# Inputs loaded transposed and split from SBUF, the memory block moved behind the projection, and the bias table read in its used order

## What is computed

```python
h, mem_n = rms_norm(x, pre_mix_g), rms_norm(mem, mem_norm_g)      # mem: 256 x 1024
q_n, k_c, v_c, k_s, v_s, k_w, v_w, g_n, q_m, k_m, v_m, q_x, gates = split(h @ w_in)
mk, mv = split(mem_n @ w_mem_kv)                                  # 4 heads of 64
# NSA, 8 heads in 2 groups: compressed, selected and window branch, each with
#   softmax(q k^T / 8 + bias_tab[t5_bucket(t - s)]) v, weighted by sigmoid(g_n)
# compress(k) = gelu((windows of 32 of k + pos) @ w1) @ w2, 15 windows
# MoBA, 4 heads, causal, same bias table (32 buckets x 12 heads); memory attention, 4 heads, no bias
merged = sum(sigmoid(gate_i) * (branch_i @ w_i_o))
x = x + rms_norm(merged @ w_mix_out, post_mix_g)
h = rms_norm(x, pre_ffn_g)
x = x + rms_norm((silu(h @ w_gate) * (h @ w_up)) @ w_down, post_ffn_g)
```

## Time and profile before

| | |
|---|---|
| median of 3 runs | 458.23 us (457.31 to 458.83) |
| the profiled execution | 457.53 us, its span 455.7 us |
| PE busy | 438.6 us (96% of the span) |
| DVE, ACT, POOL busy | 275.2, 240.5, 48.9 us |
| granted TensorE clock, mean | 0.997 of full |
| HBM read and written | 76.4 and 1.07 MB, 170 GB/s over the span |

### The profile page before, as it was taken

One profiled execution on the slowest core, in us unless ns is written; L12 is line 12 of the kernel. 1 busy time (PEld: TensorE's weight loads), 2 busy tenths in 40 slices (PEclk: granted clock), 3 DMA queues, 4 the chain that ended last, 5 costly groups with the idle time before them and its releaser, 6 DMA issues.

```text
span 455.7 us, 5968 instructions
## 1 busy us (share of the span) xinstructions
PE 438.6 (96%) x2096; PEld 351.9 (77%) x2096; DVE 275.2 (60%) x476; ACT 240.5 (53%) x412; POOL 48.9 (11%) x80
## 2 busy tenths in 40 slices
PE   3999999989999999999999989999999999999995
PEld 3776889977777777777778768888888888888883
DVE  2773893699565656754696666555555555545433
ACT  4673952377765556563436648444444444534321
POOL 5030000002112121120610230000000000000000
PEclk9999999999999999999999999999999999999998
DMA  8899825253534422335655364766555665555102
GB/s 283 312 377 324 265 89 186 92 177 100 180 98 119 159 95 92 94 95 182 235 180 185 118 205 147 236 188 186 189 183 187 189 184 184 180 182 184 74 0 92
DMA packets 50880, 77.79 MB, mean 171 GB/s; under 512 B 2068, under 2 KB 27372, under 8 KB 50856
## 3 DMA queue, kind: packets, MB, share of 16 engines
q1 hardware_dynamic: 49272, 73.07, 49.0%
q0 software_dynamic: 1424, 4.34, 2.9%
q10 hardware_dynamic: 160, 0.07, 0.1%
HBM read 76.40 MB, written 1.07 MB: 170 GB/s over the span
## 4 chain that ended last, share of the span: by engine, by line
PE 90%; DVE 3%; ACT 2%; DMA 2%; issue 1%; POOL 0%; POOLq 0%; SPq 0%; DVEq 0%; ACTq 0%
PE acc L1104 25%; PE acc L1106 24%; PE acc L1105 24%; PE ob L1351 3%; PE sbank L1274 2%; PE ptb L1325 2%; DMA mems<-in_mem 2%; PE ob L1258 2%; PE ob L1353 1%; PE sbank L1275 1%; PE ptb L1430 1%; ACT wh L459 1%; PE ob L1340 1%; DVE wl L728 1%; DVE gates L940 1%
## 5 line engine op out<-in xcount | busy, mean ns | idle before, releaser
L728 DVE TENSOR_TENSOR wl<-raw,wh 128x1024 fp32r<-128x1024 f32 (+1 forms) x130 | 158.7, 1227 | 84.8 <-ACT wh L459 84.1
L459 ACT ACTIVATE wh<-raw 128x1024 fp32r<-128x1024 f32 (+1 forms) x130 | 135.3, 1046 | 94.6 <-PE acc L1106 87.1
L1104 PE MATMUL acc<-wh,xh 128*128 128x512 f32 (+1 forms) x384 | 152.1, 396 | 0.2 <-DVE xl L758 0.2
L1106 PE MATMUL acc<-wh,xl 128*128 128x512 f32 (+1 forms) x384 | 148.6, 387 | 0.0
L1105 PE MATMUL acc<-wl,xh 128*128 128x512 f32 (+1 forms) x384 | 148.1, 386 | 0.0
L1106 PEld LDWEIGHTS acc<-wh,xl 128*128 128x128 f32 x384 | 72.1, 188 | 15.0
L1104 PEld LDWEIGHTS acc<-wh,xh 128*128 128x128 f32 x384 | 72.2, 188 | 14.4 <-issue 1.4
L1105 PEld LDWEIGHTS acc<-wl,xh 128*128 128x128 f32 x384 | 72.3, 188 | 13.3 <-issue 0.5
L1104 PE MATMUL acc<-wh,ah 128*128 128x512 f32 x88 | 34.9, 397 | 0.0
L1106 PE MATMUL acc<-wh,al 128*128 128x512 f32 x88 | 34.9, 396 | 0.0
L1105 PE MATMUL acc<-wl,ah 128*128 128x512 f32 x88 | 34.8, 396 | 0.0
(11 more groups left out here) (215 smaller groups left out, 466.3 us busy)
## 6 DMA issues: line engine op xcount, KB each, us to landing
raw<-in_w_in SPq DMA_DIRECT2D x20, 1024.0 KB
raw<-in_w_ffn_gate SPq DMA_DIRECT2D x22, 512.0 KB
raw<-in_w_ffn_up SPq DMA_DIRECT2D x22, 512.0 KB
raw<-in_w_ffn_down SPq DMA_DIRECT2D x22, 512.0 KB
raw<-in_w_mix_out SPq DMA_DIRECT2D x4, 1024.0 KB
bp<-g_scratch SPq DMA_DIRECT2D x1, 2304.0 KB, 8.5
raw<-in_w_nsa_o SPq DMA_DIRECT2D x2, 1024.0 KB
raw<-in_w_in SPq DMA_DIRECT2D x2, 560.0 KB
```

Of the source, the lines that this page charges most:

```text
L459: nc.scalar.activation(wh[:, k, :, 0:w], raw[:, slot, 2 * half:2 * half + 2, 0:w], ACT.Copy).then_inc(hi_done, 1)
L728: nc.vector.tensor_tensor(wl[:, k, :, 0:w], raw[:, slot, 2 * half:2 * half + 2, 0:w], wh[:, k, :, 0:w].bitcast(F32), ALU.subtract).then_in ...
L1104: nc.tensor.matmul(bank[:, 0:w], h[:, k, c], wh[:, slot, s, 0:w], start=first, stop=False)
L1106: return nc.tensor.matmul(bank[:, 0:w], l[:, k, c], wh[:, slot, s, 0:w], start=False, stop=last)
```

## The change

- **Inputs.** `x` and `mem` are also given transposed (`xt`, `memt`), the gains as columns (`gains`), the positions transposed (`post`). The splits read `xt0` and `memt0` in SBUF; PE's transposes of them, of the gains and of the positions are gone. `x0` and `mems` are still loaded, for the sums of squares, which ACT and DVE now take one token tile each.
- **Order of the blocks.** The projection becomes blocks 0 to 4 (subs 0 to 19, block 4 with 280 columns), memory keys and values block 5 (subs 20 to 23). The batches of queries and keys move with them: those of the projection are 0 to 6, that of the memory keys is the last, behind the first gate sub. `compress_1`, `compress_2` and the compressed scores move into block 5.
- **Bias table.** The row has 256 distances behind 127 masked ones; SP loads it back as `tb` directly (1.5 MB), the adds read it backwards, POOL copies the compressed branch's values out of it. The table products and their copies are gone, and `w1` waits for block 0 instead of `bp`.
- **First sub** in two pieces of one row group, each with loads and splits of its own.

```diff
# SP
-            for c in range(2):
-                sp.dma_start(mems[:, :, SLICE * c:SLICE * c + SLICE],
...
+            for s in range(2):
+                sp.dma_start(raw[:, 0, s], w_in[:, s, 0:SLICE]).then_inc(sub0d[s], 16)
+            sp.dma_start(xt0[:, 2:4], xt[:, 2:4]).then_inc(xtd[2], 16)
+            sp.dma_start(raw[:, 0, 2:4], w_in[:, 2:4, 0:SLICE]).then_inc(loaded[0], 32)
+            sp.dma_start(xt0[:, 4:8], xt[:, 4:8]).then_inc(xtd[3], 16)
+            plain(1, w_in, 4, 0)
+            plain(2, w_in, 0, SLICE)
+            plain(3, w_in, 4, SLICE)
             sp.dma_start(x0[:], xf).then_inc(xd, 16)
...
+            projection(2)
             sp.wait_ge(grow_done, 2)
             sp.dma_start(g_scratch, grow[:]).then_inc(g_stored, 16)
+            sp.dma_start(memt0[:], memt).then_inc(memtd, 16)
+            projection(3)
+            sp.dma_start(mems[:], memf).then_inc(memd, 16)
+            projection(4)
             sp.wait_ge(g_stored, 16)
-            sp.dma_start(bp[:], bass.AP(g_scratch.tensor, 0, [[1, P], [G_W, BIAS_H], [1, BP_W]])).then_inc(bp_d, 16)
+            sp.dma_start(tb[:], bass.AP(g_scratch.tensor, 0, [[1, P], [G_W, BIAS_H], [1, SEQ]])).then_inc(tb_d, 16)
# POOL
-            pool.wait_ge(bp_d, 16)
+            pool.wait_ge(mm_done, 4)
...
+            pool.wait_ge(tb_d, 16)
+            pool.wait_ge(zeroed, 3)
+            for t, seen in ((0, 7), (1, NCMP)):
+                src = tb[:, 0:NSA_H, 96 + P * t:97 + P * t]
+                nc.gpsimd.tensor_copy(tbc[:, t, :, 0:seen],
+                                      bass.AP(src.tensor, src.offset, [src.ap[0], [SEQ, NSA_H], [-CMP_STRIDE, seen]])
+                                      ).then_inc(tbc_done, 1)
# ACT
+            nc.scalar.dma_start(gcol[:], a["gains"]).then_inc(gaind, 16)
+            for s in range(2):
+                nc.scalar.dma_start(xt0[:, s], xt[:, s]).then_inc(xtd[s], 16)
...
+            for s in range(2):
+                x_hi(s)
+                first_hi(s)
+            split[0] = 1
+            for v in range(1, 4):
+                x_hi(2 * v)
+                x_hi(2 * v + 1)
+                hi_to(v)
+            hi_to(6)
+            act.wait_ge(xd, 16)
+            squares_of(1, x0, 0)
...
             evac_cols(2)
+            hi_to(15)
+            act.wait_ge(memtd, 16)
+            for k in range(4):
+                mem_hi(k)
+            hi_to(16)
+            high_qk(3)
+            for k in range(4, KD):
+                mem_hi(k)
             evac_cols(3)
             hi_to(20)
+            act.wait_ge(memd, 16)
+            squares_of(0, mems, 0)
+            act.wait_ge(ssq_done, 4)
+            roots(0)
+            nc.scalar.preload_act_table(ACT.Tanh)
             high_qk(4)
             evac_cols(4)
+            high_qk(5)
...
             hi_to(24)
             high_qk(6)
+            act.wait_ge(cmp_dve, 1)
+            nc.scalar.activation(hx[:, 2, :], hx[:, 1, :], ACT.Tanh, ...).then_inc(cmp_act, 1)
             evac_cols(5)
# DVE: the same order with x_lo, first_lo, mem_lo, lo_to, low_qk; the gelu stands behind low_qk(6)
-                            nc.vector.tensor_tensor(sx[:, n % 2, c0:c1], sbank[:, n % 2, c0:c1], tb[:, bh, 128 * (1 - t):256],
+                            nc.vector.tensor_tensor(sx[:, n % 2, c0:c1], sbank[:, n % 2, c0:c1], tb[:, bh, c1 - c0 - 1::-1],
# PE
+            def first_sub():
+                for s in range(2):
+                    pe.wait_ge(hi_done, s + 1)
+                    for t in range(TILES):
+                        nc.tensor.matmul(acc[:, 0, t], xh[:, s, P * t:P * t + P], wh[:, 0, s], start=(s == 0), stop=False)
+                    pe.wait_ge(xl_done, s + 1)
+                    pe.wait_ge(lo_done, s + 1)
+                    for t in range(TILES):
+                        nc.tensor.matmul(acc[:, 0, t], xh[:, s, P * t:P * t + P], wl[:, 0, s], start=False, stop=False)
+                        ins = nc.tensor.matmul(acc[:, 0, t], xl[:, s, P * t:P * t + P], wh[:, 0, s], start=False, stop=False)
+                ins.then_inc(mm_done, 1)
...
+            first_sub()
+            whole_block(0, 0, 4, xh, xl, ready=x_ready, after={1: [relative_bias]}, first=1)
+            whole_block(1, 4, 4, xh, xl)
+            whole_block(2, 8, 4, xh, xl, after={0: [lambda: qk_batch(0, 1, [col(C_Q), col(C_Q + P)])],
+                                                1: [lambda: qk_batch(1, 1, [col(C_Q + 2 * P), col(C_Q + 3 * P)])],
+                                                3: [lambda: qk_batch(2, 2, [col(C_KC), col(C_VC)])]})
+            whole_block(3, 12, 4, xh, xl, after={1: [lambda: qk_batch(3, 3, [col(C_KS), col(C_KW)])]})
+            whole_block(4, 16, 4, xh, xl, w=ATT_TAIL,
+                        after={1: [lambda: qk_batch(4, 4, [col(C_QM), col(C_QM + P)])],
+                               3: [lambda: qk_batch(5, 4, [col(C_KM), col(C_KM + P)])]})
+            whole_block(5, 20, 4, memh, meml, ready=mem_ready,
+                        after={0: [lambda: compress_1(0), lambda: compress_1(1)],
+                               1: [lambda: compress_1(2), lambda: qk_batch(6, 5, [col(C_QX), col(C_QX + P)])],
+                               2: [compress_2],
+                               3: [lambda: compressed_scores(0), lambda: compressed_scores(1)]})
```

More of the change, by code:

```diff
@@ L146, in build_layer @@
         xh = sb("xh", [P, KD, SEQ], F32R)
+        with ExitStack() as early:
+            xt0 = sb("xt0", [P, KD, SEQ], F32, early)
         xl = sb("xl", [P, KD, SEQ], F32R)
@@ L158, in build_layer @@
             memh = sb("memh", [P, KD, SEQ], F32R, s)
+            with ExitStack() as early:
+                memt0 = sb("memt0", [P, KD, SEQ], F32, early)
             meml = sb("meml", [P, KD, SEQ], F32R, s)
             mems = sb("mems", [P, TILES, D], F32, s)
[L161 to L165, removed]
         gates = sb("gates", [P, TILES, 3 * D])
@@ L340, in _ @@
+            for half in range(2):
+                plain(2 * B_MEMKV + half, w_memkv, 4 * half, 0)
+            u = 2 * B_GATE
             for gate_blocks, w in (((0, 1, 2, 3), w_moba), ((4, 5), w_mem)):
@@ L788, in _ @@
-            dve.wait_ge(memd[0], 16)
-            dve.wait_ge(memd[1], 16)
-            for t in range(TILES):
-                round_lo(1, t)
-                nc.vector.tensor_tensor_reduce(out=junk[:, t], in0=mems[:, t], in1=mems[:, t], scale=1.0, scalar=0.0, op0=ALU.mult,
-                                               op1=ALU.add, accum_out=ssq[:, 0, t:t + 1]).then_inc(ssq_done, 1)
-            lo_to(4)
-            for j in (2, 3):
-                round_lo(1, j)
+            for s in range(2):
+                x_lo(s)
+                first_lo(s)
@@ new lines, in _ @@
+            split[0] = 1
+            for v in range(1, 4):
+                x_lo(2 * v)
+                x_lo(2 * v + 1)
+                lo_to(v)
+            dve.wait_ge(bias_row, 1)
+            nc.vector.tensor_scalar(grow[:, MASK_W:MASK_W + SEQ], ob[0:BIAS_H, 0:SEQ], 1.0 / SCALE, None,
+                                    ALU.mult).then_inc(grow_done, 1)
+            nc.vector.memset(grow[:, 0:MASK_W], MASKED / SCALE)
+            nc.vector.memset(grow[:, MASK_W + SEQ:G_W], 0.0).then_inc(grow_done, 1)
@@ L871, in _ @@
             ins.then_inc(cmp_g, 1)
+            lo_to(15)
+            for k in range(4):
+                mem_lo(k)
+            lo_to(16)
+            dve.wait_ge(zeroed, 1)
+            low_qk(3)
+            for k in range(4, KD):
+                mem_lo(k)
             evac_cols(3)
             lo_to(20)
+            dve.wait_ge(memd, 16)
+            squares_of(0, mems, 1)
             low_qk(4)
-            lo_to(21)
+            dve.wait_ge(root_done, 2)
+            reciprocals(0, 0)
+            dve.wait_ge(rstd_done, 2)
+            evac_cols(4)
+            low_qk(5)
+            dve.wait_ge(cmp_act, 1)
+            link(nc.vector.tensor_scalar(gsig[:], gsig[:], 0.5, 0.5, ALU.mult, ALU.add))
+            gview = gsig[:].rearrange("p t (h b) -> p t h b", b=3)
+            lo_to(24)
+            low_qk(6)
             dve.wait_ge(cmp_pe, 1)
```

369 lines of the change are left out of this document (132 added, 237 removed).

## The result

The changed kernel takes 452.27 us (median of 4 executions, 451.15 to 454.38), the kernel before 458.42 beside it (457.31 to 458.83). The ratio of the comparison is 0.9887, 95% interval 0.9867 to 0.9907: faster by 1.1%, some 5 to 6 us, where 10 were forecast. The profiled execution took 451.15 us, 6.4 less than that of before.

The account below looks back on a forecast made before the run. PE bounds the kernel, busy 438.6 of 455.7 us. Gains 4.1 + 8.8 + 1.5 less costs 0.9 + 0.6 + 0.5 + 2.0 + 0.4 make 10.0 us: 448 us forecast, range 446 to 450.

Parts of the forecast that it names:

- My rate: Start: a flow from 2 us passes the first 396 KB by 3.7, landed at 5.7 us with 1.9 added.
- 1.6 stood: Start: eight products at 0.43 us before 0.23 comes cost 1.6, less 0.7 the kernel before had: net 0.9.
- the 0.6: Start: PE, free at 11.1 us, waits for sub 1, split by 11.7; cost 0.6.
- the 8.8 us: PE work removed: transposes, gains, positions and bias tables, 9.5 us, less 0.7 for an added bias product; gain 8.8.
- over 10 us of cover: Projection loads: SP's new waits delay only weight units 6 and up, wanted after 38 us, so no cost.
- That is even; I take 0: Projection blocks 2 to 4: DVE needs 13.5 us until sub 17 is split, PE gets there in 13.6; cost 0.
- The rival of a lag of ACT and DVE: Blocks 3 to 5: ACT and DVE fall behind without pauses, 4 us more of waits, 452; chance 0.07.
- only change place: Moved query/key transposes, 64 compress_1 products and score products change place only; no term in the 8.8 us gain.
- the forecast 2.0 us wait at `compress_2`: Block 5: PE, ready at 15.7 us from block start, waits for the hidden layer until 17.7; cost 2.0.
- 0.4 forecast: Block 5: DVE's split of sub 25, ckeys and vcz end at 21.5, PE's sub 23 at 21.1; cost 0.4.
- The backward read: Bias adds in the jobs: reading backwards costs 0, DVE adds stay 0.35 us; slower-than-before rival, chance 0.03.
- its sum of 9: Total gain if POOL's tbc copies and DVE's SBUF splits shut each other out, sub 17 up to 1 us late.

Follow-up runs that it names:

- e2: First part of compress_1 moved behind block 4, so no 44 small products follow each other, against the changed kernel: 450.13 us, 3.0 less by the ratio.
- e7: Later loads of memt0 and mems plus compress_1 and gelu earlier, against the changed kernel: 444.68 us, 1.7% less.
- e3: Loads of memt0 and mems one block of weights later on SP's queue, against the changed kernel: 449.71 us, 3.7 less by the ratio.
- e5: POOL issues the w1 loads behind sub 11 instead of sub 3, against the changed kernel: 449.89 us, 3.2 less by the ratio.
- e6: compress_1 parts behind subs 18, 19 and 20, gelu ahead of batch 6, against the changed kernel: 447.56 us, 4.9 less by the ratio.
- e1: The changed kernel timed again without edits, as base of the other runs: 452.98 us.
- e9: First sub started whole instead of in two pieces, against the changed kernel: 453.14 us, 0.5 more by the ratio.
- e8: Six fp32 table products put back on PE in block 1, result unused, against the changed kernel: 453.51 us, 1.7 more by the ratio.
- e4: First compress_1 part behind block 4 and memt0, mems loaded later, together, against the changed kernel: 447.35 us, 5.5 less by the ratio.
- e11: Six table products put back into the kernel with later loads and earlier gelu: 449.98 us against 444.68.
- e12: First sub started whole in the kernel with later loads and earlier gelu: 447.21 us against 444.68.
- e10: All 64 products of compress_1 in one row behind sub 20, against the changed kernel: 454.69 us, 2.2 more by the ratio.

## Why the prediction was half right

**The start: right in sum, two terms off.** First product at 6.14 (6.75 forecast): the weight piece, issued at 0.76, landed 3.2 us later, at 4.0, and ACT's rounding of the first x piece waited for `xt0` until 5.1. My rate gave 5.7 for the later of the two, between 5.2 and 6.5; it came at my lower end. The Trainium skill ("DMA: Bandwidth & Descriptors", Anatomy of one DMA), whose figures are for loads that GpSimd issues, gave 3.7; this trace does not agree. Low level: 14 steps instead of 8, to 12.25, which cost 2.85 (6.1 less 14 at 0.233) where 1.6 stood. The clock column reads 1.00 there, as it does in the earlier trace rows; at the start the level is read from the steps alone. In return PE was slow enough to find sub 1 ready, so the 0.6 did not occur, and sub 2 began at 15.18, 0.5 earlier than the forecast's 15.7. That two misses cancel is luck: the same start has 9 low steps in the profile of e2, and in e7, with 9, PE did wait 0.6 for sub 1.

**PE work removed: the 8.8 us were right as work**, wrong as time. PE's busy time fell by 8.7; the 3.8 us that PE worked ahead of its first split product, gone as well, and some 3.8 us more at the low level (2.2 at the start, 1.6 behind the small products) cancel in that. The step that failed is "SP's new waits (for `grow`, at 18.5, then `memt0`, `mems`, `tb`) have units 6 and up behind them, wanted after 38 us: over 10 us of cover." I asked when SP would issue the units, not how many bytes were then ahead of them. The 12.8 MB worked out above give, at the 402 GB/s of the earlier trace rows, 9 + (12.8 - 2.3)/0.402 + 1.9 = 37 us, against the 36.2 at which ACT wanted the unit: no cover at all. And all parts of this were in the diff: SP's list, PE's earlier work, and POOL's `w1`, which hangs on `mm_done` and so moved from 30.2 to 21.2 us. e3 and e5 take away bytes at two different queues, and the waits at subs 15 and 17 go (0.2 is left at sub 17 in e5). The forecast said that it would be wrong if PE waited over 2 us in blocks 3 and 4: it waited 2.6.

**Blocks 3 and 4:** "That is even; I take 0. Each us that DVE is later is a us of PE" was right as a sensitivity. The row of DVE work was as counted; it began late, because unit 6 did, and subs 15 and 17 paid 1.1 and 1.5. The rival of a lag of ACT and DVE has such waits too, and its 452 is the measured time, but by luck: its reason (no pauses left) is not what e3, e5 and e7 show. In e7 PE has fewer pauses still, and in blocks 3 and 4 it waits for no split.

**Clock: the missing term.** I costed the level at the start alone. Moved `compress_1` parts "only change place", I wrote; 44 in a row where there had been 22 cost 1.6 us behind them, and the forecast 2.0 us wait at `compress_2` brought about as much again in some executions. In e2 the first is gone, in e6 both. In five of the six profiles with 44 in a row the level fell at their end or before it (the changed kernel, e1, e3, e5, e9), for 6 to 12 split products, and not in e8; with no more than 22 in a row (e2, e4, e6, e7, e11, e12) never there. So the row is shown as what brings it here, but not that it must.

**`compress_2` and the scores: right.** The wait is 1.98 (2.0 forecast), released by `hidv`; none at the first scores. The compressed scores begin at 88.86, 0.2 us after the step of sub 23's last product would have ended (0.4 forecast), released by DVE's copy of `pat`. **The backward read: right**, 350 ns against 351. **x0 and the queries of the other batches: right**, no wait of PE came from them.

**Splits from SBUF beside POOL.** A split of x took 0.48 us from SBUF, as it had from PSUM. Four splits of the memory tokens began while POOL's copies of `tbc` still ran and took 1.84 us together, the other four 1.67:

```profile
53.03 1.42 POOL L412 COPY tbc<-tb 128x56 f32<-128x56 f32 x2 [8.37 <-DMA tb<-g_scratch]
53.69 1.84 DVE L799 SCALAR_TENSOR_TENSOR meml<-memt,gcol,memh 128x256 fp32r<-128x256 f32 x4
```

That is 0.2 us, and in e3 and e7 sub 17 waited for nothing. The Trainium skill ("SBUF — State Buffer", Who interferes with whom) says that such a pair of instructions shut each other out; the 1 us at sub 17 that the forecast worked out from it, and its sum of 9, are not borne out.

**The sum for the profiled execution:** 10.0 forecast, 0.5 more at the start, 0.2 more at the compressed scores, 2.6 less for the late splits, 1.6 less for the clock: 6.5, measured 6.4. The median lies another 1.1 above it; by the profile of e1, with the low level in two places, I take that for a second dip in some executions. That is argued from one profile and the mean clocks, not from a trace of each execution.

What stays open is the clock: why the level falls behind the wait of 2.0 us at `compress_2` in six profiles (e1, e2, e3, e8, e9, e10) and not in three (the changed kernel, e4, e5), and why 44 small products in a row did not bring it down in e8. The 3.5 of 5.2 us that e8 gives back are no riddle beside this: 2.6 of waits for splits and 1.6 of the low level behind the small products are gone from its profile, and e1, the base, had both.

## What to carry to other kernels

When a change pulls PE's work forward and DMA engines are full, sum the bytes of all queues ahead of each weight unit and divide by the measured rate; a place in the queue says nothing. PE work removed ahead of a late load is given back in part (1.7 of 5.2 us kept, some of the rest by the clock), and counts in full once the loads come in time (5.3), so put the loads in the order of need first. And don't stack small products: three parts between full subs cost nothing, two together cost 1.6 us behind them in the first profile, and three together another 2.2 us.

## What was not expected of the hardware

- PE busy for 1.00 of each window, but with products of 30 columns, fell from the 2.4 to the 1.2 GHz level: at the end of 44 of them (4.8 to 5.5 us) in five of six profiles, during 64 of them in the one profile of e10, behind 22 (2.4 us) never in the profiles here.
- A wait of PE of 2.0 us was followed by the low level in six of the nine profiles that have it at `compress_2`, and once at sub 15 (e2).
- The low level after a start from rest lasted 14 steps, 6.1 us, from PE's first product, and 9 steps in another execution with the same start (e2); in the kernel before, which had transposed ahead of it, three.
- With several queues full the rate was 359 GB/s over 29 us, at a DMA share of 1.05 (402 in the earlier trace rows); 1 MB loads of SP's queue took 14 to 20 us from issue to landing, in the profile of the changed kernel:

```profile
memt<-in_memt SPq DMA_DIRECT2D x1, 1024.0 KB, 19.7
...
x<-in_x SPq DMA_DIRECT2D x1, 1024.0 KB, 14.4
...
raw<-in_w_in SPq DMA_DIRECT2D x2, 256.0 KB, 3.2
```
